# Hybrid attention and mLSTM block: who splits the attention's keys and queries into parts, and when they are stored

## The chip, the cores and the metric

One core of one Trainium2 chip runs the kernel. The time is the device time of one execution in microseconds; the median of several executions is compared.

## The reference

One layer on a sequence of 512 rows of width 1024. The input is normalised, multiplied by a wide matrix (1024 x 4616) and the product is split into nine groups of 512 columns (attention queries, keys, values and gate; mLSTM queries, keys, values, output gate and gate) and 8 gate columns. Cut to what matters:

```python
h = rms_norm(x, pre_norm_g[l])
proj = jnp.einsum('bsd,dc->bsc', h, w_in[l])
aq, ak, av, az, mq, mk, mv, mo, mz, mi, mf = split_columns(proj)
ya = moba_attention(partial_rope(att_heads(aq), pos), partial_rope(att_heads(ak), pos), att_heads(av))
ya = rms_norm(ya, attn_out_g[l]) * jax.nn.silu(az)
qk = jax.nn.silu(causal_depthwise_conv(jnp.concatenate([mq, mk], axis=-1), conv_w[l], conv_b[l]))
hm = mlstm_chunkwise(...)
ym = jax.nn.sigmoid(mo) * hm * jax.nn.silu(mz)
y = jnp.einsum('bsc,cd->bsd', jnp.concatenate([ya, ym], axis=-1), w_out[l])
x = x + rms_norm(y, post_norm_g[l])
```

Attention has 8 heads of 64; with this length every query sees all earlier rows. The mLSTM has 4 heads of 128.

## The kernel before

Every product is done in two parts of each operand: a high part, which is the number rounded to what TensorE reads, and a low part, which is the rest. A product is then three matmuls, high x high, high x low, low x high (`product`, L1497 to L1499, or in another order). For weights, ScalarE copies the raw tile into `w_hi` (`cut`, L817) and VectorE subtracts it from the raw tile to get `w_lo` (`cut`, L1068). GpSimd does this subtraction for the weight slots from 64 on (L662, L666).

The work is ordered by slots, written out by hand. A slot is one weight tile of 128 x 512: 88 in all. SyncE issues the load of slot n into one of 4 raw buffers once the low part of slot n-4 is done. ScalarE and VectorE run a loop over b and cut slot b+6 in step b. TensorE multiplies slot b in step b. So SyncE's slot n comes at about the time of VectorE's step n-10. Slots 0 to 7 are the mLSTM values. Then, for each head of the mLSTM, come four slots with its queries and keys (from 8, 20, 32 and 44) and eight slots of the attention: gate (12 to 19), keys (24 to 31), queries (36 to 43), values (48 to 55). `PARTS_AT` is (36, 48), the first slot behind the keys' and the queries' group and the next head's four. From slot 56 come the mLSTM gates, and with slot 62 the attention begins.

Around the change these things run in each head h of the mLSTM:

- VectorE: `conv_in` and `conv` (L1160, L1171, L1173 three times) for the head's queries (n = 2h) and keys (n = 2h+1), `qk_low(n)` (L1182) after ScalarE's silu (L884) and high copy (L888), `weighted(h, j)` (L1193), which reads the scores of tile j from PSUM and multiplies by the decay, `pm_low` (L1202), `head_sum` (L1210), `head_stats` (L1222 to L1234) and `head_norm` (L1240, L1242).
- TensorE: `head_scores(h, j)`, three matmuls after slots `ST_AT[h] + j` (40 to 43 for head 2, 52 to 55 for head 3), of 512, 384, 256 and 128 columns. It waits for `qk_low(2h+1)` and for `weighted` of the tile before. `head_values` in the four slots behind.
- GpSimd: `decay_rows(h)` (four DMAs, L641), `head_rsqrt(n)` (L624, the root for two tiles, for which `head_norm` waits), `decay_mask(h)` (four small additions, L648).

The attention's keys and queries: `kq_rows(w, m)` (w = 0 keys, 1 queries; m = 0 to 3 blocks of dimensions; L1253 to L1261) takes the projection out of PSUM, with the rotation for m = 0, into `by_dims`, which is the tile `stage`. ScalarE copies each to `by_dims_hi` (`kq_high`, L903), which is half of the tile `gy`. VectorE subtracts in place (`kq_low`, L1266). SyncE stores both parts to DRAM (`rows_out`, L528), and GpSimd's queue reads them back as `keys`, `queries` and `swapped` (L676, L685, L703, L706) in the arrangement that the attention needs. As queries use the same tiles as keys, `kq_rows(1, 0)` waits until all eight stores of the keys have landed (`kq_out[0]`).

Before, `PARTS_IN` says in which step the parts are taken, ScalarE one step ahead of VectorE, and SyncE stores them 11 slots behind:

```python
PARTS_IN = ({0: (0,), 2: (1,), 4: (2, 3)}, {4: (0, 1), 5: (2, 3)})
OUT_BEHIND = 11
```

ScalarE: m = 0 in step 35, 1 in 37, 2 and 3 in 39; queries 0 and 1 in 51, 2 and 3 in 52. VectorE: steps 36, 38, 40, 40 and 52, 52, 53, 53. SyncE: slots 47, 49, 51, 51 and 63, 63, 64, 64.

Of the kernel before, what the change touches and what calls it, by code (L numbers as in the profile page):

```python
# [18 lines left out]
F32 = mybir.dt.float32  # L19
F32R = mybir.dt.float32r  # L20
ALU = mybir.AluOpType
# [5 lines left out]
NT = SEQ // P  # L27
# [3 lines left out]
MH, MD = 4, 128  # L31
# [74 lines left out]
PE_ST = {ST_AT[h] + j: (h, j) for h in range(MH) for j in range(NT)}  # L106
PE_PV = {ST_AT[h] + NT + t: (h, t) for h in range(MH) for t in range(NT)}
PARTS_AT = (S_AQ, S_AV)
PARTS_IN = ({0: (0,), 2: (1,), 4: (2, 3)}, {4: (0, 1), 5: (2, 3)})
OUT_BEHIND = 11  # L110
FIRST_Q = 3
LAST_SLOT = S_MO - 2

# [109 lines left out]
def build(nc, x, pre_g, w_in, i_bias, f_bias, conv_w, conv_b, attn_g, mlstm_g, w_out, post_g, rope, out):  # L223
    with ExitStack() as ctx:
# [3 lines left out]
        def sem(name):  # L228
            return ctx.enter_context(nc.semaphore(name))
# [81 lines left out]
        by_dims, by_dims_hi = stage, gate.bitcast(F32R)  # L311
        by_dims_lo = stage[:].bitcast(F32R)
# [104 lines left out]
        conv_done = sem("conv_done")  # L417
# [33 lines left out]
        kq_hi = sem("kq_hi")  # L451
        kq_lo = sem("kq_lo")
# [42 lines left out]
        def low_done(eng, n):  # L495

            eng.wait_ge(w_lo_done[n % 2], n // 2 + 1)
# [4 lines left out]
        def turn_tile(n):  # L502

            _, kind, i = TURNS[n]
            return 0 if kind == "ym" else 4, NT - 1 - i
# [9 lines left out]
        @block.sync  # L515
        def _(sp):
            x2 = x.rearrange("b s d -> (b s) d")

            def load_x(c):
                k, n = X_CHUNKS[c]  # L520
                cols = slice(k * P, (k + n) * P)
                sp.dma_start(x_sb[:, :, cols], x2[:, cols].rearrange("(t p) d -> p t d", p=P)).then_inc(x_in[c], 16)

            def rows_out(w, m):

                for q, (done, src) in enumerate(((kq_hi, gate), (kq_lo, by_dims))):
                    sp.wait_ge(done, NT * w + m + 1)
                    sp.dma_start(kq_dram[w, :, q, ROT * m:ROT * m + ROT, :], src[:, m, :]).then_inc(kq_out[w], 16)  # L528

            for n, (mat, kind, k, c) in enumerate(SLOTS):  # L530
                if n in X_BEFORE:
                    load_x(X_BEFORE[n])
                if n >= RAW:
                    low_done(sp, n - RAW)
                w = w_in if mat == "in" else w_out
                if kind == "cols":
                    src = w[0, k * P:(k + 1) * P, c:c + AW]
                    dst = w_raw[:, n % RAW, :]
                else:
                    src = w[0, k * P:(k + 4) * P, c:c + MD].rearrange("(k p) c -> p k c", p=P)  # L540
                    dst = w_raw[:, n % RAW, :].rearrange("p (k c) -> p k c", k=4)
                sp.dma_start(dst, src).then_inc(raw_in[n % RAW], 16)
                if n == NK - 1:
                    sp.dma_start(wg_raw[:], w_in[0, :, MG:MG + 8].rearrange("(k p) c -> p k c", p=P)).then_inc(wg_in, 16)
                if n == S_QK + 6:
                    sp.wait_ge(ssx_done, NT)
                    sp.dma_start(gains[:], attn_g.to_broadcast([P, AW])).then_inc(gain_in, 16)
                for w in range(2):
                    for m in PARTS_IN[w].get(n - OUT_BEHIND - PARTS_AT[w], ()):
                        rows_out(w, m)  # L550
                if n == S_AQ + 4:
                    sp.wait_ge(az_gained, NT)
                    sp.dma_start(gains[:], mlstm_g.to_broadcast([P, AW])).then_inc(gain_in, 16)
            sp.wait_ge(kq_out[1], 32 * NT)
            sp.dma_start(post, post_g.to_broadcast([P, D])).then_inc(post_in, 16)

            def load_residual(i):
                t = NT - 1 - i
                sp.dma_start(xr[i], x2[t * P:(t + 1) * P, :]).then_inc(xr_in[i], 16)

            sp.wait_ge(ym_gated, NT)
            load_residual(0)
            load_residual(1)
            sp.wait_ge(turn_ps, TURN_OF["ym", NT - 1] + 1)
            load_residual(2)
            load_residual(3)
            store(sp, 0)
            store(sp, 1)
            store(sp, 2)
            sp.wait_ge(out_ready, 2 * NT - 1)  # L570
            sp.dma_start(out[0, 0:P, 0:AW], xr[NT - 1][:, 0:AW]).then_inc(out_done[NT - 1], 16)
            sp.wait_ge(out_ready, 2 * NT + 1)
            sp.dma_start(out[0, 0:P, quarter[1]], xr[NT - 1][:, quarter[1]]).then_inc(out_done[NT - 1], 16)
            for i in range(NT):
                sp.wait_ge(out_done[i], 32 + 16 * (i == NT - 1))
# [3 lines left out]
        def _(g):  # L579
# [43 lines left out]
            def rsqrt(dst, src):  # L623
                return g.tensor_tensor(dst, src, mhalf[:, 0:src.shape[1]], ALU.pow)  # L624
# [19 lines left out]
            def decay_mask(h):  # L644
                g.wait_ge(g_back, 16 * NT * (h + 1))
                for j in range(NT):
                    v = decay[j][:, 0:P]
                    g.tensor_tensor(v, v, causalT[:], ALU.add).then_inc(g_masked, 1)  # L648

            def head_rsqrt(n):  # L650
                g.wait_ge(var_done, n + 1)
                rsqrt(vr[:], vs2[:]).then_inc(vr_done, 1)

            def cut(n):
# [9 lines left out]
                else:  # L664
                    hi, lo = out_home(n - S_OUT)
                    g.tensor_tensor(lo, blocks(w_raw[:, n % RAW, :]), hi.bitcast(F32),  # L666
                                    ALU.subtract).then_inc(w_lo_done[n % 2], 1)

            def head_rows(w, h):

                return kq_dram[w, h].rearrange("q d s -> (q d) s")
# [47 lines left out]
            for h in range(1, MH):  # L719
                decay_rows(h)  # L720
                head_rsqrt(2 * h - 2)
                if h == MH - 1:
                    for n in range(AH):
                        keys_back(n)
                decay_mask(h)
                head_rsqrt(2 * h - 1)
            swapped_back(3)
            for h in range(FIRST_Q):
                queries_back(h)
# [76 lines left out]
        def _(a):  # L806
# [110 lines left out]
            for b in range(S_QK, LAST_SLOT + 1):  # L917
                if b == S_QK:
                    cut(b + AHEAD - 2)
                    cut(b + AHEAD - 1)  # L920
                if b == S_MZ + 1:
                    for t in range(NT):
                        v_high(t)
                cut(b + AHEAD)
                if b == S_QK:
                    a.wait_ge(onep_done, 1)
                    a.activation(rows[0], rows[2], ACT.Ln).then_inc(ln_done, 1)
                if b == S_QK + 1:
                    rope_scale()
                if b == S_QK + 5:  # L930
                    rope_evac()
                if b == S_QK + 3:
                    a.wait_ge(gmax_done, 1)
                    a.activation(gate_rows[32:48, :], rows[2], ACT.Copy, scale=-1.0).then_inc(gneg_done, 1)
                if b == ST_AT[0]:
                    a.wait_ge(aT_done, 1)
                    a.activation(emt[:], bank[7][:].rearrange("p (t c) -> p t c", t=NT)[:, :, 32:32 + MH],
                                 ACT.Exp).then_inc(emt_done, 1)
                for h in range(MH):
                    if b - 2 in PE_ST and PE_ST[b - 2][0] == h:  # L940
                        pm_high(*PE_ST[b - 2])
                    for c in range(2):
                        if b == S_Q[h] + 2 * c + 5:
                            conv_silu(2 * h + c)
                        if b == ST_AT[h] + c:
                            decays(h, 2 * c)
                            decays(h, 2 * c + 1)
                for c in range(2):
                    for t in (2 * c, 2 * c + 1):
                        if b == S_AK - 3 + c:  # L950
                            az_evac(a, t)
                for w in range(2):
                    for m in PARTS_IN[w].get(b + 1 - PARTS_AT[w], ()):
                        kq_high(w, m)

            def out_cut(n):
# [38 lines left out]
            for s in range(STEPS):  # L995
# [20 lines left out]
                for kind, what in events:  # L1016
# [7 lines left out]
                    elif kind == "y_sq":  # L1024
                        i, c = what
                        n = OUT_OF[i, c]
# [21 lines left out]
        def _(v):  # L1048
# [8 lines left out]
            def f32(ap):  # L1057
                return ap.bitcast(F32)
# [202 lines left out]
                v.tensor_tensor(by_dims[:, 0, :], by_dims[:, 0, :], turned, ALU.add).then_inc(kq_ready, 1)  # L1261
                v.wait_ge(kq_ready, NT * w + 1)

            def kq_low(w, m):
                v.wait_ge(kq_hi, NT * w + m + 1)
                v.tensor_tensor(by_dims_lo[:, m, :], by_dims[:, m, :], f32(by_dims_hi[:, m, :]),  # L1266
                                ALU.subtract).then_inc(kq_lo, 1)

            def v_low(t):
                part = v_hl[:, t * AH:(t + 1) * AH]  # L1270
                v.wait_ge(v_hi_done, t + 1)
# [4 lines left out]
            for b in range(S_QK, LAST_SLOT + 1):  # L1276
# [29 lines left out]
                for c in range(2):  # L1306
                    for m in (2 * c, 2 * c + 1):
                        if b == S_AQ - 3 + (m > 0):
                            kq_rows(0, m)
                        if b == S_AV - 3 + (m > 0):  # L1310
                            kq_rows(1, m)
                for w in range(2):
                    for m in PARTS_IN[w].get(b - PARTS_AT[w], ()):
                        kq_low(w, m)
                if b - 2 in PE_PV and PE_PV[b - 2][1] % 2 == 1:
                    head_stats(2 * PE_PV[b - 2][0] + PE_PV[b - 2][1] // 2)
                for h in range(MH):
# [562 lines left out]
```

## Time and profile before

| what | us |
|---|---|
| median of 3 runs | 322.23 (321.74 to 324.36) |
| the profiled execution, its own time | 323.46 |
| its span, first to last instruction | 321.5 |
| TensorE busy | 311.0 |
| VectorE busy | 224.6 |
| ScalarE busy | 163.0 |
| GpSimd busy | 109.2 |

The engines are PE (TensorE), DVE (VectorE), ACT (ScalarE), POOL (GpSimd) and SP (SyncE, which only issues DMAs). Times in the profile are microseconds from the start of the span. A busy engine is not always a bound one; the records of matmuls overlap, so the pace is read from their starts. The granted clock is 1.00 at TensorE's full speed and 0.50 at half of it.

### The profile page before, as it was taken

Reading aid. Unit: us, or ns where it says so; the run is one execution under the profiler, and the core shown is the slowest. Engines: PE = TensorE matmul, PEld = TensorE weight load, DVE = VectorE, ACT = ScalarE, POOL = GpSimd, SP = SyncE. Lnnn points to the kernel's source line nnn. Section 1 sums busy time; section 2 is a strip of 40 time slices with the busy share of each in tenths; the row PEclk is TensorE's granted clock in tenths of the full one; section 3 lists DMA queues with packets and bytes.
Section 4 is the critical chain, followed back from the end, with each engine's and each line's share of the span. In section 5 each row is a group of like instructions: output and inputs, shape, how many; then the busy total and the mean of one; then the engine's idle time right before and its main releaser. Section 6 shows DMA issues by size and latency. Waiting matters only on the chain.

```text
span 321.5 us, 4954 instructions
## 1 busy us (share of the span) xinstructions
PE 311.0 (97%) x1567; PEld 260.6 (81%) x1567; DVE 224.6 (70%) x508; ACT 163.0 (51%) x332; POOL 109.2 (34%) x144
## 2 busy tenths in 40 slices
PE   8999999999999999999998799999999999999992
PEld 4888888888888888888886688888888898888892
DVE  3544999658997799966997576654677586966534
ACT  4358947486373326742329261274566976452301
POOL 8201006228240231002550008796443888000000
PEclk9999999999999999999999599999999999999997
DMA  7931544863835563479583569591018376310111
GB/s 240 298 100 33 164 135 113 199 176 97 134 83 158 135 113 95 117 224 232 138 260 98 172 236 246 147 214 66 34 35 130 109 257 162 131 67 0 65 67 65
DMA packets 35576, 44.58 MB, mean 139 GB/s; under 512 B 3976, under 2 KB 19632, under 8 KB 35552
## 3 DMA queue, kind: packets, MB, share of 16 engines
q1 hardware_dynamic: 27360, 34.51, 35.2%
q0 software_dynamic: 8032, 9.63, 17.6%
q8 instruction: 13, 0.21, 0.3%
q10 hardware_dynamic: 160, 0.14, 0.1%
q14 instruction: 11, 0.09, 0.1%
HBM read 37.88 MB, written 6.39 MB: 138 GB/s over the span
## 4 chain that ended last, share of the span: by engine, by line
PE 71%; DVE 14%; issue 6%; DMA 4%; ACT 3%; SPq 1%; DVEq 0%; POOLq 0%; POOL 0%; ACTq 0%
PE bank L1497 18%; PE bank L1499 17%; PE bank L1498 17%; PE bank L1545 4%; DVE farena L1173 3%; PE bank L1830 3%; PE bank L1798 3%; DMA kq_rows<-stage 2%; DVE w_lo L1068 2%; PE bank L1779 2%; PE bank L1780 2%; DMA w_raw<-in_w_in 1%; PE bank L1729 1%; DVE stage L1253 1%; PE bank L1526 1%
## 5 line engine op out<-in xcount | busy, mean ns | idle before, releaser
L817 ACT ACTIVATE w_hi<-w_raw 128x512 fp32r<-128x512 f32 x71 | 43.7, 626 | 65.9 <-PE bank L1499 56.1
L1497 PE MATMUL bank<-w_hi,xT_hi 128*128 128x512 f32 (+1 forms) x180 | 73.3, 407 | 0.0
L1499 PE MATMUL bank<-w_hi,xT_lo 128*128 128x512 f32 (+1 forms) x180 | 70.7, 393 | 0.0
L1498 PE MATMUL bank<-w_lo,xT_hi 128*128 128x512 f32 (+1 forms) x180 | 70.3, 391 | 0.0
L1068 DVE TENSOR_TENSOR w_lo<-w_raw,w_hi 128x512 fp32r<-128x512 f32 x64 | 46.0, 729 | 8.7 <-ACT w_hi L817 8.6
L1497 PE MATMUL bank<-xT_hi,w_hi 128*128 128x512 f32 x128 | 50.8, 397 | 0.0
L1499 PE MATMUL bank<-xT_hi,w_lo 128*128 128x512 f32 x128 | 50.1, 392 | 0.0
L1498 PE MATMUL bank<-xT_lo,w_hi 128*128 128x512 f32 x128 | 50.0, 390 | 0.0
L1499 PEld LDWEIGHTS bank<-w_hi,xT_lo 128*128 128x128 f32 x180 | 34.4, 191 | 7.4
L1498 PEld LDWEIGHTS bank<-w_lo,xT_hi 128*128 128x128 f32 x180 | 34.6, 192 | 5.8
L1497 PEld LDWEIGHTS bank<-w_hi,xT_hi 128*128 128x128 f32 x180 | 34.5, 192 | 5.6
L1372 DVE CUSTOM_DVE_ANT_0 farena<-bank,causal 128x512 f32<-128x512 f32 (+3 forms) x32 | 15.7, 489 | 19.6 <-PE bank L1780 19.5
L1499 PEld LDWEIGHTS bank<-xT_hi,w_lo 128*128 128x128 f32 x128 | 24.0, 188 | 5.3
L1497 PEld LDWEIGHTS bank<-xT_hi,w_hi 128*128 128x128 f32 x128 | 24.1, 188 | 4.4
L1498 PEld LDWEIGHTS bank<-xT_lo,w_hi 128*128 128x128 f32 x128 | 24.1, 188 | 4.4
L993 ACT ACTIVATE rarena<-bank 128x512 fp32r<-128x512 f32 (+3 forms) x32 | 13.9, 434 | 20.1 <-PE bank L1830 20.0
L1378 DVE TENSOR_TENSOR rarena<-bank,rarena 128x512 fp32r<-128x512 f32 (+3 forms) x32 | 15.6, 487 | 6.3 <-ACT rarena L993 5.6
L641 POOL DMA_DIRECT2D farena<-g_rows x16 | 9.0, 568 | 31.3 <-DVE farena L1193 29.6
L1173 DVE SCALAR_TENSOR_TENSOR farena<-farena,pcol 128x512 f32<-128x512 f32 x24 | 18.4, 769 | 0.8
L985 ACT ACTIVATE farena<-farena,mx 128x512 f32<-128x512 f32 (+3 forms) x32 | 17.9, 560 | 1.1 <-DVE mx L1372 1.0
L1193 DVE SCALAR_TENSOR_TENSOR farena<-bank,farena 128x512 f32<-128x512 f32 (+3 forms) x16 | 7.8, 488 | 14.9 <-PE bank L1499 14.9
L624 POOL TENSOR_TENSOR vr<-vs,mhalf 128x2 f32<-128x2 f32 x8 | 5.7, 712 | 34.7 <-DVE vs L1232 34.7
(217 smaller groups left out, 613.4 us busy)
## 6 DMA issues: line engine op xcount, KB each, us to landing
w_raw<-in_w_in SPq DMA_DIRECT2D x72, 256.0 KB, 3.3
rarena<-kq_rows POOLq DMA_DIRECT2D x20, 256.0 KB, 4.5
w_raw<-in_w_out SPq DMA_DIRECT2D x16, 256.0 KB, 2.8
kq_rows<-gy SPq DMA_DIRECT2D x8, 256.0 KB
kq_rows<-stage SPq DMA_DIRECT2D x8, 256.0 KB
gy<-in_x SPq DMA_DIRECT2D x4, 512.0 KB, 3.9
out_y<-gy SPq DMA_DIRECT2D x7, 256.0 KB, 2.0
farena<-in_x SPq DMA_DIRECT2D x4, 256.0 KB, 4.2
```

What stands on the lines that cost most here:

```text
L817: a.activation(hi, raw, ACT.Copy).then_inc(w_hi_done, 1)
L985: a.activation(prob[:, s % 2, 0:n], sm[:, s % 2, 0:n], ACT.Exp, scale=-1.0, bias=mx[:, s:s + 1], accum_out=rsum[:, s:s + 1]).then_inc(prob ...
L993: a.activation(pT[:, 2 * (u % 2), 0:n], bank[4 + u % 2][:, 0:n], ACT.Copy).then_inc(pt_hi, 1)
L1068: v.tensor_tensor(lo, raw, hi, ALU.subtract).then_inc(w_lo_done[n % 2], 1)
L1173: ins = v.scalar_tensor_tensor(out=acc, in0=u[:, j:j + SEQ], scalar=tap[j], in1=acc, op0=ALU.mult, op1=ALU.add)
L1372: v.tensor_tensor_reduce(sm[:, s % 2, 0:n], bank[6 + s % 2][:, 0:n], causal[:, SEQ - n:], -Q_SCALE, BIG, ALU.add, ALU.min, mx[:, s:s + 1]) ...
L1378: v.tensor_tensor(pT[:, 2 * (u % 2) + 1, 0:n], bank[4 + u % 2][:, 0:n], f32(pT[:, 2 * (u % 2), 0:n]), ALU.subtract).then_inc(pt_lo, 1)
L1497: pe.matmul(o, hi, m_hi, start=start, stop=False)
L1498: pe.matmul(o, hi, m_lo, start=False, stop=False)
L1499: return pe.matmul(o, lo, m_hi, start=False, stop=stop)
L1545: mm = pe.matmul(bank[t][:], xs[:, k, t * P:(t + 1) * P], ws, start=k + term == 0, stop=False)
L1798: mm = pe.matmul(bank[2][:, 2 * P * (u % 2):2 * P * (u % 2 + 1)], v_hl[:, j * AH + h, :], pT[:, 2 * (u % 2):2 * (u % 2) + 2, j * P:(j + 1) ...
```

## The change

The high parts are taken by ScalarE in steps given by `HIGH_IN`: keys in 34 (m = 0) and 35 (1, 2, 3), queries in 47 (0, 1) and 48 (2, 3). The low parts are taken by GpSimd: for keys, m = 0 to 2 behind the mask of head 2 and m = 3 behind the root that follows; for queries all four, once the last convolution is done. The stores go out at SyncE's slots in `OUT_IN`: keys 46, 47, 47, 48, queries 61, 61, 62, 62.

```diff
-PARTS_IN = ({0: (0,), 2: (1,), 4: (2, 3)}, {4: (0, 1), 5: (2, 3)})
-OUT_BEHIND = 11
+HIGH_IN = ({-2: (0,), -1: (1, 2, 3)}, {-1: (0, 1), 0: (2, 3)})
+OUT_IN = ({10: (0,), 11: (1, 2), 12: (3,)}, {13: (0, 1), 14: (2, 3)})
@@ sync
-                    for m in PARTS_IN[w].get(n - OUT_BEHIND - PARTS_AT[w], ()):
+                    for m in OUT_IN[w].get(n - PARTS_AT[w], ()):
                         rows_out(w, m)
@@ gpsimd
+            def kq_low(w, m):
+                g.wait_ge(kq_hi, NT * w + m + 1)
+                g.tensor_tensor(by_dims_lo[:, m, :], by_dims[:, m, :], by_dims_hi[:, m, :].bitcast(F32),
+                                ALU.subtract).then_inc(kq_lo, 1)
...
                 decay_mask(h)
+                if h == MH - 2:
+                    for m in range(NT - 1):
+                        kq_low(0, m)
                 head_rsqrt(2 * h - 1)
+                if h == MH - 2:
+                    kq_low(0, NT - 1)
+            g.wait_ge(conv_done, 2 * MH)
+            for m in range(NT):
+                kq_low(1, m)
             swapped_back(3)
@@ scalar
-                    for m in PARTS_IN[w].get(b + 1 - PARTS_AT[w], ()):
+                    for m in HIGH_IN[w].get(b - PARTS_AT[w], ()):
                         kq_high(w, m)
@@ vector
-            def kq_low(w, m):
-                v.wait_ge(kq_hi, NT * w + m + 1)
-                v.tensor_tensor(by_dims_lo[:, m, :], by_dims[:, m, :], f32(by_dims_hi[:, m, :]),
-                                ALU.subtract).then_inc(kq_lo, 1)
...
-                for w in range(2):
-                    for m in PARTS_IN[w].get(b - PARTS_AT[w], ()):
-                        kq_low(w, m)
```

## Rows read from the trace of the kernel before

**Rows 1.** The page: busy time of the engines, and the chain that ended last.

```profile
PE 311.0 (97%) x1567; PEld 260.6 (81%) x1567; DVE 224.6 (70%) x508; ACT 163.0 (51%) x332; POOL 109.2 (34%) x144
...
PE 71%; DVE 14%; issue 6%; DMA 4%; ACT 3%; SPq 1%; DVEq 0%; POOLq 0%; POOL 0%; ACTq 0%
```

**Rows 2.** Stages: length, busy PE, PEld, DVE, ACT, POOL, granted clock, DMA share, GB/s.

```profile
176.00:178.00 2.00, 0.16 (x1) 0.00 (x0) 1.69 (x3) 1.49 (x4) 0.00 (x0) 1.00 0.01 2
178.00:179.00 1.00, 0.05 (x1) 0.08 (x1) 1.00 (x3) 0.16 (x1) 0.00 (x0) 0.60 0.92 229
179.00:184.00 5.00, 5.00 (x13) 4.13 (x14) 2.16 (x4) 1.51 (x3) 0.00 (x0) 0.50 0.63 200
```

**Rows 3.** Timeline of PE: start, duration; in brackets idle time before, and its releaser.

```profile
134.93 0.39 PE L1497 MATMUL bank<-rarena 128*128 128x512 f32 x1
...
138.36 0.34 PE L1497 MATMUL bank<-rarena 128*128 128x384 f32 x1
...
141.62 0.28 PE L1497 MATMUL bank<-rarena 128*128 128x256 f32 x1
...
172.44 0.50 PE L1497 MATMUL bank<-rarena 128*128 128x512 f32 x1 [0.19 <-DVE rarena L1182]
...
178.95 0.66 PE L1497 MATMUL bank<-rarena 128*128 128x384 f32 x1 [2.78 <-DVE farena L1193]
...
185.11 0.28 PE L1497 MATMUL bank<-rarena 128*128 128x256 f32 x1
```

**Rows 4.** The chain that ended last, in order of time: start, length, what.

```profile
140.05 8.00 DMA kq_rows<-stage
...
174.71 1.04 ACT gy L903 x2
```

**Rows 5.** Timeline of DVE from 145 to 179.

```profile
145.77 0.68 DVE L1068 TENSOR_TENSOR w_lo<-w_raw,w_hi 128x512 fp32r<-128x512 f32 x1
148.24 0.69 DVE L1258 TENSOR_TENSOR stage<-bank,farena 128x512 f32<-128x512 f32 x1 [1.79 <-DMA kq_rows<-stage]
...
166.95 2.33 DVE L1173 SCALAR_TENSOR_TENSOR farena<-farena,pcol 128x512 f32<-128x512 f32 x3
...
171.71 0.68 DVE L1182 TENSOR_TENSOR rarena<-farena,rarena 128x512 fp32r<-128x512 f32 x1
...
176.31 0.69 DVE L1068 TENSOR_TENSOR w_lo<-w_raw,w_hi 128x512 fp32r<-128x512 f32 x1 [2.11 <-ACT w_hi L817]
176.91 1.29 DVE L1266 TENSOR_TENSOR stage<-stage,gy 128x512 fp32r<-128x512 f32 x2
```

**Rows 6.** Groups by line and shape: count, busy us, mean ns, idle before.

```profile
L1266 DVE TENSOR_TENSOR stage<-stage,gy 128x512 fp32r<-128x512 f32 x8 | 5.2, 684 | 0.0
...
L662 POOL TENSOR_TENSOR w_lo<-w_raw,w_hi 128x512 fp32r<-128x512 f32 x8 | 10.4, 1327 | 0.4 <-ACT w_hi L817 0.4
```

**Rows 7.** Timelines of POOL and DVE where both work in SBUF.

```profile
73.46 6.00 POOL L718 TENSOR_TENSOR silu_az<-silu_az,gains 128x512 f32<-128x512 f32 x4 [4.67 <-ACT silu_az L786]
...
75.09 1.78 DVE L1068 TENSOR_TENSOR w_lo<-w_raw,w_hi 128x512 fp32r<-128x512 f32 x1
...
78.23 1.77 DVE L1068 TENSOR_TENSOR w_lo<-w_raw,w_hi 128x512 fp32r<-128x512 f32 x1
...
195.80 2.62 DVE L1224 SCALAR_TENSOR_TENSOR den<-num,emt 128x2 f32<-128x2 f32 x1
...
195.81 2.58 POOL L662 TENSOR_TENSOR w_lo<-w_raw,w_hi 128x512 fp32r<-128x512 f32 x2
```

**Rows 8.** Timelines of POOL and DVE around both parts.

```profile
118.34 2.78 POOL L648 TENSOR_TENSOR farena<-farena,causalT 128x128 f32<-128x128 f32 x4
...
133.40 0.68 DVE L1182 TENSOR_TENSOR rarena<-farena,rarena 128x512 fp32r<-128x512 f32 x1
...
192.76 1.44 POOL L703 DMA_DIRECT2D wg<-kq_rows  x2 [26.43 <-DMA kq_rows<-stage]
```

**Rows 9.** Timeline of SP: the first store of the queries' parts.

```profile
177.40 0.59 SPq L528 DMA_DIRECT2D kq_rows<-gy  x1
```

## The prediction, with its working

> **What bounds the kernel now.** I read the page's busy shares and its chain first, then the stages by window, then the timelines of the four engines around the one place where TensorE stands still. TensorE is busy for 97% of the span and is 71% of the chain that ended last [rows 1]. Its products leave it at an even pace from the first weights to the last, so only two things can shorten the run: fewer products (the change removes none), or fewer waits and slow-clock stretches of TensorE. The stages show one such place [rows 2]: from 176 to 178 TensorE is busy for 0.16 of 2 us, in 178 to 179 the granted clock goes from 1.00 to 0.60, and from 179 to 184 it is 0.50, the lower of its two levels (1.2 instead of 2.4 GHz).
>
> The timeline of TensorE gives the prices [rows 3]. It waits 0.19 us before the scores of head 3, tile 0 (at 172.44, for VectorE's `qk_low`), and 2.78 us before the scores of tile 1 (at 178.95, for VectorE's `weighted`). The stretch from there to the scores of tile 2 took 185.11 - 178.95 = 6.16 us at the lower clock; the same products for head 2, at the higher one, took 141.62 - 138.36 = 3.26 us. So the clock cost 2.90 us, and the place as a whole 0.19 + 2.78 + 2.90 = 5.87 us. That is what can be had.
>
> Why is VectorE late there? The chain of waits [rows 4] goes back through ScalarE's weight copy and, in front of it, its last two `kq_high` copies (174.71), and further back through VectorE without a gap to 148.24, where VectorE had waited 1.79 us for the last store of the keys to land [rows 4, 5] (issued by SyncE, 8.00 us until it landed). `kq_rows(1, 0)` can't overwrite the shared tile before that. Close to the stall VectorE idled 2.11 us at 176.31 for ScalarE's weight copy and then did two `kq_low` ahead of `weighted` [rows 5].
>
> **The change, part by part.** Times are those of the profiled execution: span 321.5, its own time 323.46, so 1.96 lie around the span. The median of the runs shown is 322.23, 1.23 less; I put the differences on that median.
>
> ScalarE's eight `kq_high` are issued sooner: the first part in schedule slots 34 and 35 instead of 35, 37 and 39, the second in 47 and 48 instead of 51 and 52. None is added. At the new places ScalarE mostly waits for TensorE to free a weight buffer, so they cost nothing there; if that cover were gone they would cost 0.6 us each. The last two stood in the chain in front of the weight copy for 1.04 us [rows 4], and two more stood before the same head's silu table and decays; that goes. With the DMA wait gone as well, I expect the copy that VectorE waited for some 3 us sooner (2 x 1.04 and part of the 1.79), so the wait of 2.11 us goes whole.
>
> VectorE's eight `kq_low` go: 0.68 us each as a record, 0.6 by start to start [rows 5, 6]. Two stood between the keys' rows and `qk_low` of head 2's keys, so 1.2 us come off that path. Four (the second part) stood between `qk_low(7)` and `weighted(3, 0)`: 2.4 us.
>
> SyncE's stores: by slot number they are only 1 to 3 slots sooner for the first part (46, 47, 48 for 47, 49, 51) and 2 sooner for the second (61, 62 for 63, 64); the same sixteen DMAs. The first part's last store was issued at 140.05 [rows 4]. Slot 48 comes when VectorE has cut slot 44's weights, which stands two operations ahead of `qk_low(5)` at 133.40 [rows 8]: 132 plus whatever VectorE is late, say 134; GpSimd must have cut block 3 as well, about 130. So the last store is issued at about 136 and lands, with the same 8.00 us, at 144, before 146.4, when VectorE is through the cut at 145.77 [rows 5]. The 1.8 us wait goes. What is late next is nothing: VectorE is busy without a gap until 169.28, so the end of the last convolution moves from there (166.95 + 2.33) to 167.5 [rows 5]. The weight loads of SyncE behind the stores move by the width of four issues (0.6 us each), in front of ScalarE's copies that are six slots ahead: nothing. The second part's stores went out from 177.4 on [rows 9]; now from about 173. GpSimd's reloads of queries follow sooner, and TensorE didn't wait for them before, so that is worth nothing either.
>
> GpSimd's eight `kq_low`. A subtraction of that size takes it 1.33 us [rows 6], so 4 x 1.3 = 5.2 us for each part. GpSimd has the time: it idles for 26.43 us up to 192.76 [rows 8]. Behind them in its queue stand the root for head 1 (between the third and the fourth) and, for the second part, only reloads that wait for these very parts. The cost is elsewhere. While GpSimd multiplied four tiles at 73.46, VectorE's subtractions took 1.78 and 1.77 us instead of 0.69 [rows 7]: 1.1 us lost for each GpSimd operation that meets a VectorE operation with two inputs in SBUF. At 195.80 a VectorE operation on two columns took 2.62 us, the whole of two GpSimd subtractions (2.58) [rows 7]. So a moved part costs VectorE between 0 (when VectorE is idle or reads one input) and 1.3 us, against 0.6 saved. I take 1.1, since these are the same operations on the same sizes.
>
> The Trainium skill has this as a rule, and it speaks against the change (SBUF, State Buffer, section "Who interferes with whom"): the second port pair of VectorE is GpSimd's, it is an exclusive lock, and a VectorE instruction with two SBUF inputs and a GpSimd instruction that reads SBUF block each other, whichever comes second for the whole length of the first. The trace agrees in kind; by the rule's whole length the price would be 1.3 us per operation, 5.2 us per part instead of 4.4.
>
> Second part, where it decides. `kq_low(1, .)` waits for the last convolution, 167.5, and so starts in the very moment when VectorE has `qk_low(6)`, a normalisation, two weight cuts and `qk_low(7)` to do: 3.1 us from 169.28 to 172.39 before [rows 5]. Now 167.5 + 3.1 = 170.6 without contention. TensorE wants `qk_low(7)` at 172.44 - 0.19 = 172.25 [rows 3], so there are 1.65 us of slack. Four operations at 1.1 are 4.4; about 0.75 of that lies beside the normalisation, which reads one tile. 170.6 + 3.65 = 174.25: TensorE waits 2.0 us before the scores of tile 0. (Bounds: 0, if GpSimd loses each race, and 170.6 + 5.2 - 172.25 = 3.5.) The next wait, for `weighted`, goes: TensorE came to it 178.95 - 2.78 - 172.44 = 3.73 us after the start of the first scores [rows 3], so now at 178.0, and VectorE, with two cuts at 0.6 in front, is there at 175.5.
>
> First part: GpSimd is free when the masks of head 2 are done (118.34 + 2.78 = 121.1), three subtractions follow, the fourth after the root at about 129 [rows 8]. VectorE there has convolutions (two SBUF inputs) but also reductions from PSUM and statistics; laying the two timelines side by side I get 2.4 us of the 4.4. Less the 1.2 saved, `qk_low(5)` ends 1.2 later than its 134.08 (133.40 + 0.68) [rows 8]; TensorE asks at 134.93 [rows 3]. So a new wait of 0.35 us (bounds 0 and 5.2 - 1.2 - 0.85 = 3.2).
>
> Sum: waits 0.35 + 2.0 = 2.35 instead of 2.97. And the clock? It fell when TensorE had stood for about 2.2 us (last product done at about 176.2, fall in the slice 178 to 179) [rows 2, 3], and it did not fall after 0.19. A wait of 2.0 is shorter than what had passed when it fell, so I take it that the clock stays, by a narrow margin. Then 5.87 - 2.35 = 3.5 us are gained: 318.7 (own time of a profiled execution about 320).
>
> **The rivals.**
> A, the wait is only moved and the clock falls again: 0.35 + 2.0 + 2.9 = 5.25 against 5.87, so -0.6: 321.6. For it: the margin of the clock is 0.2 us. Against: the shorter wait.
> B, contention is small because GpSimd's reads fall into VectorE's gaps and one-input operations: no wait, no slow clock, -5.9: 316.4. For it: 1.65 us of slack and the 2.11 us of idle VectorE; against: the dense stretch after the convolution.
> C, the port decides the other way, in the first part: if VectorE loses more than 2.05 us (1.2 saved + 0.85 slack) between 121 and 134, TensorE waits there; at the whole 4.4 that is 2.35 us, with the clock falling 2.9 more, and the second part, with nothing beside the normalisation, at 170.6 + 4.4 - 172.25 = 2.8, and again 2.9. 10.95 against 5.87: +5.1, 327.3, slower. For it: the one operation that was held up by two. Against: the reductions and statistics between.
> D, the change doesn't do what it says: the keys' last store still lands too late, since by slots it is only three sooner and behind GpSimd's root. Then the 1.8 us stay and all of the second part is later by it: 0.35 + 3.8 + 2.9 = 7.05, +1.2: 323.4. Against: some 2 us of margin.
>
> **How the numbers follow.** Forecast 0.36, A 0.24, B 0.24, C 0.10, D 0.06. A measurement of this kernel tells about 1%, 3.2 us, from no change. Faster by more than that (below 319.0): all of B and three quarters of the forecast, 0.51. Slower (above 325.5): most of C and a little of D, 0.10. Within: 0.39. The range 316.0 to 323.0 holds the forecast, A and B with a little on both sides, and leaves out C and half of D.
>
> **What would show it.** Right: the wait for the DMA at `kq_rows(1, 0)` is gone; GpSimd's eight subtractions have 1.3 to 1.8 us each; VectorE's `w_lo` cuts beside them have 1.1 us more than 0.69; TensorE waits some 2 us for `qk_low(7)` (line of head scores) and no longer for `weighted`; the granted clock stays 1.00 there. Wrong: VectorE's records around 168 to 174 no longer than before (then B); a TensorE wait near 135, or the clock at 0.50 there (C); VectorE still waiting for a DMA near 147 (D). A wait of TensorE after 200 that isn't there now would upset all of it.

## The result, and the profile after

The changed kernel takes 325.54 us (median of 13 executions, 324.36 to 328.18), the kernel before 322.21 beside it (13 executions). The ratio is 1.0109, with an interval of 1.0081 to 1.0136: slower by 1.1%. The forecast was 318.7, faster. Ratios here and below leave out executions more than 1.5% above the fastest of their kernel, among them one of e10 that took 796.13 us, 2.5 times as long as its others, for a reason that no run shows.

In the profiled executions the span went from 321.5 to 323.6 us, and the own time from 323.46 to 325.68. TensorE's timeline after the change answers to [rows 3]. The columns are start and duration, and in brackets the idle time before and who ended it.

```profile
136.85 0.50 PE L1502 MATMUL bank<-rarena 128*128 128x512 f32 x1 [1.83 <-DVE rarena L1195]
...
141.98 0.34 PE L1502 MATMUL bank<-rarena 128*128 128x384 f32 x1
...
178.57 0.58 PE L1502 MATMUL bank<-rarena 128*128 128x512 f32 x1 [2.69 <-DVE rarena L1195]
...
183.70 0.34 PE L1502 MATMUL bank<-rarena 128*128 128x384 f32 x1
```

There are now two places instead of one. Both are the first scores of a head (2 and 3), and both wait for `qk_low` (L1195, was L1182). The wait of 2.78 us for `weighted` is gone. The granted clock fell in both places, as its rows by stage show (columns as in [rows 2]):

```profile
137.00:138.00 1.00, 1.00 (x5) 0.83 (x6) 0.40 (x1) 1.00 (x3) 0.00 (x0) 0.94 0.81 307
138.00:141.00 3.00, 3.00 (x9) 2.32 (x8) 1.29 (x2) 1.65 (x5) 0.00 (x0) 0.50 0.68 223
141.00:143.00 2.00, 2.00 (x11) 1.69 (x10) 0.98 (x2) 0.79 (x2) 0.00 (x0) 0.92 0.89 257
176.00:178.00 2.00, 0.00 (x0) 0.00 (x0) 2.00 (x3) 0.89 (x3) 0.76 (x1) 1.00 0.00 0
178.00:179.00 1.00, 0.43 (x2) 0.35 (x3) 1.00 (x2) 0.00 (x0) 0.00 (x0) 0.93 0.57 117
179.00:181.00 2.00, 2.00 (x6) 1.59 (x5) 1.68 (x4) 0.87 (x2) 0.00 (x0) 0.50 0.83 260
```

Each place takes 5.13 us from its first scores to the scores of the next tile (141.98 - 136.85 and 183.70 - 178.57). The same work at full clock took 138.36 - 134.93 = 3.43 us for head 2 [rows 3], and for head 3 as much in e9 below (172.71 to 176.14). So each clock fall cost 1.70 us, and the two places together cost 1.83 + 1.70 + 2.69 + 1.70 = 7.92 us. The one place before cost 5.87. The difference, 2.05, is the whole of what the span grew by (2.1). The medians differ by 3.3. The profiled execution of before lay 1.25 above its median, that of after 0.14 above, and the remaining 1.2 us are in executions of which there is no trace. The likely reason is the clock. The profiled execution of before had a mean granted clock of 0.984, lower than any of the 52 executions of that kernel that were run beside the experiments (0.988 to 0.996), while that of after, 0.987, lies among its own kernel's (0.984 to 0.993). So an ordinary execution of before probably lost less than the 5.87 us of this trace. That is argued from the means, which also hold the last few us of each span, at 0.50, and is not shown by a trace.

Why is `qk_low` late? VectorE's timeline up to it, in both places:

```profile
121.53 1.25 DVE L1253 TENSOR_TENSOR hsc<-vr,iden 128x2 f32<-128x2 f32 x1
122.82 2.53 DVE L1255 TENSOR_SCALAR gy<-num,mva,hsc 128x128 f32<-128x128 f32 x2
...
129.82 1.50 DVE L1184 TENSOR_SCALAR farena<-farena,pcol 128x512 f32<-128x512 f32 x1
...
168.96 2.33 DVE L1186 SCALAR_TENSOR_TENSOR farena<-farena,pcol 128x512 f32<-128x512 f32 x3
171.20 0.69 DVE L1195 TENSOR_TENSOR rarena<-farena,rarena 128x512 fp32r<-128x512 f32 x1
171.81 1.25 DVE L1253 TENSOR_TENSOR hsc<-vr,iden 128x2 f32<-128x2 f32 x1
173.10 2.52 DVE L1255 TENSOR_SCALAR gy<-num,mva,hsc 128x128 f32<-128x128 f32 x2
175.54 2.37 DVE L1081 TENSOR_TENSOR w_lo<-w_raw,w_hi 128x512 fp32r<-128x512 f32 x2
177.84 0.68 DVE L1195 TENSOR_TENSOR rarena<-farena,rarena 128x512 fp32r<-128x512 f32 x1
```

And GpSimd's at the same times:

```profile
121.03 4.24 POOL L671 TENSOR_TENSOR stage<-stage,gy 128x512 fp32r<-128x512 f32 x3
...
129.74 1.30 POOL L671 TENSOR_TENSOR stage<-stage,gy 128x512 fp32r<-128x512 f32 x1
...
171.37 5.40 POOL L671 TENSOR_TENSOR stage<-stage,gy 128x512 fp32r<-128x512 f32 x4 [3.03 <-DVE farena L1186]
```

A multiplication of two columns (L1253) takes 1.25 us instead of 0.15. The two normalisations behind it (L1255) take 2.53 and 2.52 as a pair instead of 0.60. Two weight cuts take 2.37 instead of 1.29, one step of the convolution (L1184) 1.50 instead of 0.55. The sum of the excess is 1.10 + 1.93 + 0.95 = 3.98 us for the keys' four subtractions and 1.10 + 1.92 + 1.08 = 4.10 us for the queries' four: 1.0 us each. Beside it VectorE saved 0.6 us each, but only two of the eight had stood ahead of `qk_low(5)`, and none ahead of `qk_low(7)`: 1.2 us saved against 3.98 in the first place, nothing against 4.10 in the second.

What the change was meant to undo did go. No row is left in which VectorE waits for the keys' store [rows 5]: after the change `kq_rows(1, 0)` starts at 150.00, straight behind the weight cut. The end of head 3's last convolution is at 171.29, where it was at 169.28, with TensorE 3.5 us later by then: 1.5 us sooner against TensorE.

### The profile page after: what moved, and what is told of

Its sections match the earlier page's. It is cut to its first block, busy times and chain, and to the rows that moved or that the text cites. A ratio compares the mean times of both kernels' runs of the same rounds, so it can differ in the third digit from the quotient of the medians.

```text
span 323.6 us, 4955 instructions
## 1 busy us (share of the span) xinstructions
PE 311.9 (96%) x1567; PEld 260.9 (81%) x1567; DVE 227.9 (70%) x500; ACT 163.0 (50%) x332; POOL 120.9 (37%) x152
## 4 chain that ended last, share of the span: by engine, by line
PE 76%; DVE 17%; issue 5%; DVEq 0%; ACT 0%; POOLq 0%; POOL 0%; ACTq 0%
PE bank L1502 19%; PE bank L1504 19%; PE bank L1503 19%; PE bank L1550 4%; DVE farena L1186 3%; PE bank L1835 3%; DVE w_lo L1081 3%; PE bank L1803 3%; DVE gy L1255 2%; PE bank L1784 2%; PE bank L1785 2%; PE bank L1531 1%; PE bank L1734 1%; DVE farena L1184 1%; PE bank L1517 1%
## 5 line engine op out<-in xcount | busy, mean ns | idle before, releaser
L1081 DVE TENSOR_TENSOR w_lo<-w_raw,w_hi 128x512 fp32r<-128x512 f32 x64 | 47.0, 747 | 13.4 <-ACT w_hi L830 13.3
L1504 PE MATMUL bank<-xT_hi,w_lo 128*128 128x512 f32 x128 | 50.8, 397 | 0.0
L1503 PE MATMUL bank<-xT_lo,w_hi 128*128 128x512 f32 x128 | 50.7, 396 | 0.0
```

The lines of the kernel that those rows point to most:

```text
L1081: v.tensor_tensor(lo, raw, hi, ALU.subtract).then_inc(w_lo_done[n % 2], 1)
L1503: pe.matmul(o, hi, m_lo, start=False, stop=False)
L1504: return pe.matmul(o, lo, m_hi, start=False, stop=stop)
```

## The experiments

Theory 1 says that VectorE is held up by GpSimd's subtractions, at the two points where TensorE waits for `qk_low`. Theory 2 says that the earlier stores and copies cost the time: SyncE or ScalarE is held up, and the weights come late. The kernel before stood at 322.77 beside e1 to e4, at 322.86 beside e5 to e8, and at 322.33 beside e9 and e10 (medians).

**e1: all low parts back on VectorE; early high parts and early stores kept.**

```diff
+LOW_IN = ({0: (0,), 1: (1, 2), 2: (3,)}, {3: (0, 1), 4: (2, 3)})
@@ vector
+                for w in range(2):
+                    for m in LOW_IN[w].get(b - PARTS_AT[w], ()):
+                        kq_low(w, m)
@@ gpsimd: the calls of kq_low taken out
```

> The changed kernel with its early high parts and early stores kept, and all eight low parts back on VectorE (keys in steps 36, 37, 37, 38, queries in 51, 51, 52, 52). Theory 1 (the loss is VectorE held up by GpSimd's subtractions, just before qk_low of heads 2 and 3): TensorE's two waits of 1.83 and 2.69 us and both clock falls go; two more low parts than before stand ahead of qk_low(5), 1.2 us against 0.85 us of slack, so a wait of about 0.35 us there: 322.2 - 5.87 + 0.35 = 316.7. Theory 2 (the loss comes from the earlier stores and copies: SyncE or ScalarE is held up and the weights come late): the time stays near 325.5 and VectorE's records have no excess.

319.58 us, ratio 0.9892 (0.9831 to 0.9953). So the change without its move to GpSimd is faster than before by 1.1%, and that same move makes it slower than before. Theory 2 falls as an account of the loss. The forecast was 3 us too low, and TensorE's timeline shows one part of that, a wait I had not seen:

```profile
135.65 0.50 PE L1503 MATMUL bank<-rarena 128*128 128x512 f32 x1 [0.26 <-DVE rarena L1188]
...
184.75 0.47 PE L1503 MATMUL bank<-w_hi,xT_hi 128*128 128x512 f32 x1 [1.24 <-DVE rarena L1278]
```

The 0.26 us were expected (0.35). The 1.24 us are TensorE waiting for the low parts of the attention's values (L1278), and ScalarE's timeline has what is in front of them (the first row is the weight copy of slot 62, the second the values' copies):

```profile
182.31 0.63 ACT L823 ACTIVATE w_hi<-w_raw 128x512 fp32r<-128x512 f32 x1 [3.79 <-DMA w_raw<-in_w_in]
...
183.15 2.41 ACT L913 ACTIVATE rarena<-bank,rx 128x512 fp32r<-128x512 f32 x4
```

ScalarE waits 3.79 us for the weights of slot 62, whose load was issued behind the queries' stores, and the values' copies (L913) stand behind that. Theory 2 has this much in it: the earlier queries' stores do cost something. These two waits are 1.5 of the 2.9 us. The rest is about what the base was off: the forecast took 5.87 us, from an execution 1.25 us above its median, off a median.

**e2: only the keys' low parts back on VectorE; e3: only the queries'.**

```diff
+LOW_IN = ({0: (0,), 1: (1, 2), 2: (3,)}, {})          # e2
+LOW_IN = ({}, {3: (0, 1), 4: (2, 3)})                 # e3
```

> As e1, but only the keys' low parts on VectorE; the queries' on GpSimd as in the change. Theory 1: only the wait before the scores of head 3 is left, 2.7 us, with a clock loss of 1.7 to 2.9 us: 316.7 + 4.4 to 5.6 = 321.1 to 322.3. Theory 2: near 325.5, as nothing is changed in stores and copies.

> As e1, but only the queries' low parts on VectorE; the keys' on GpSimd as in the change. Theory 1: only the wait before the scores of head 2 is left, 1.8 us, with a clock loss of 1.7 to 2.9 us: 322.2 - 5.87 + 3.5 to 4.7 = 319.8 to 321.0. Theory 2: near 325.5.

e2: 323.82 us, ratio 1.0020 (0.9984 to 1.0057). e3: 322.86, ratio 0.9988 (0.9949 to 1.0026). They lie 1.5 and 1.9 us above the upper end of what theory 1 expected, and both between the change and e1: each part is enough to lose what the rest gains. The traces have the waits where they should be. For e2 (first fence) head 3's scores wait for `qk_low`, and head 2's for only 0.25 us, as in e1. For e3 (second) only head 2's wait. The second wait in each is the one for the values' low parts. It explains a part of why both are above what I expected:

```profile
175.64 0.50 PE L1506 MATMUL bank<-rarena 128*128 128x512 f32 x1 [2.45 <-DVE rarena L1191]
189.34 0.77 PE L1506 MATMUL bank<-w_hi,xT_hi 128*128 128x512 f32 x1 [3.32 <-DVE rarena L1281]
```

```profile
137.31 0.50 PE L1508 MATMUL bank<-rarena 128*128 128x512 f32 x1 [1.84 <-DVE rarena L1193]
187.67 0.47 PE L1508 MATMUL bank<-w_hi,xT_hi 128*128 128x512 f32 x1 [1.16 <-DVE rarena L1283]
```

In e3 the clock fell at the first of its waits (0.50 from 139 to 141). In e2 it did not fall at the wait of 2.45 us, but at that of 3.32. This trace of e2 is of an execution of 327.17 us, 3.35 above the median, so the size of its second wait is not taken as usual.

**e4: no subtraction at all.**

```diff
-                g.tensor_tensor(by_dims_lo[:, m, :], by_dims[:, m, :], by_dims_hi[:, m, :].bitcast(F32),
-                                ALU.subtract).then_inc(kq_lo, 1)
+                g.memset(by_dims_lo[:, m, 0:1].bitcast(F32), 0.0).then_inc(kq_lo, 1)
```

> As the change, but GpSimd writes one column in place of each low part (the low parts of keys and queries are left out of the computation), so neither VectorE nor GpSimd subtracts. Theory 1: all waits of TensorE and both clock falls go, 322.2 - 5.87 = 316.3, and that is the most that moving these parts can bring. Theory 2: near 325.5.

318.62 us, ratio 0.9858 (0.9795 to 0.9922). This is as far as moving these eight subtractions can go with the stores of the change, and it is 2.3 us above what I expected. e1, which does all eight on VectorE, is only 1.0 us above it. So on VectorE they cost next to nothing once they don't stand in front of `qk_low` in a bad moment; on GpSimd they cost 7.5 us: the change is 3.33 us above the kernel before that ran beside it, e4 is 4.15 below its own. (The 1.0 us between e1 and e4 is within the spread of their four executions each.) e4 still has waits of 0.45 us for the values' low parts and 0.9 in the attention, and its miss, like that of e1, is mostly the base.

**e5: GpSimd writes for about as long as it did, but reads nothing.** Each subtraction (1.3 us) becomes two writes of zeros (0.53 us each).

```diff
-                g.tensor_tensor(by_dims_lo[:, m, :], by_dims[:, m, :], ..., ALU.subtract).then_inc(kq_lo, 1)
+                g.memset(by_dims_lo[:, m, :].bitcast(F32), 0.0).then_inc(kq_wr, 1)
+                g.wait_ge(kq_wr, NT * w + m + 1)
+                g.memset(by_dims_lo[:, m, :].bitcast(F32), 0.0).then_inc(kq_lo, 1)
```

> As the change, but each subtraction of GpSimd is replaced by two writes of zeros over the same low part, about 0.5 us each (the low parts of keys and queries are left out of the computation): GpSimd writes SBUF for about 1 us per part and reads nothing. Theory 1a (VectorE's operations with two inputs lose against GpSimd's reads, its normalisations and tensor_scalar lose because they take both of the second ports, the writing one too): the weight cuts beside it keep 0.69 us, and the two normalisations stay longer than 0.60. Theory 1b (the normalisations lost against the reads as well): everything on VectorE is as long as without GpSimd, and the time is that of the kernel without low parts, about 319.

317.99 us (one execution), as if GpSimd did nothing. VectorE beside six of the writes (121.2 to 124.5) and beside eight (167.9 to 172.3):

```profile
121.74 0.15 DVE L1255 TENSOR_TENSOR hsc<-vr,iden 128x2 f32<-128x2 f32 x1
121.92 1.01 DVE L1257 TENSOR_SCALAR gy<-num,mva,hsc 128x128 f32<-128x128 f32 x2
...
123.38 0.68 DVE L1083 TENSOR_TENSOR w_lo<-w_raw,w_hi 128x512 fp32r<-128x512 f32 x1
...
168.51 0.61 DVE L1257 TENSOR_SCALAR gy<-num,mva,hsc 128x128 f32<-128x128 f32 x2
169.05 1.28 DVE L1083 TENSOR_TENSOR w_lo<-w_raw,w_hi 128x512 fp32r<-128x512 f32 x2
```

The operations with two inputs keep 0.15 and 0.68 us. The normalisations have 1.01 in one place and 0.61 in the other, so they meet GpSimd's writes at times, at 0.4 us for a pair. Theory 1a holds for its first half and only in part for the second. For operations with two inputs it is GpSimd's reading that costs. For the normalisations the runs leave open how much is due to the reading and how much to the length of one GpSimd instruction, 1.3 us against 0.53. The Trainium skill (SBUF, State Buffer, section "Who interferes with whom") names both kinds: an instruction with two SBUF inputs contends with a GpSimd instruction that reads SBUF and not with one that only writes it, and `tensor_scalar` can enter a mode with two ports, in which it contends with GpSimd, if its operands meet that mode's conditions. The rows of the change and of e5 agree with the first, and in kind with the second; that the mode was on here, no row says. It is what I passed over when I counted the normalisation as free.

**e6: the queries' subtractions on GpSimd, but later.** As e2, with another wait and the stores behind it.

```diff
-            g.wait_ge(conv_done, 2 * MH)
+            g.wait_ge(pm_done, NT * (MH - 1) + 1)
-OUT_IN = (..., {13: (0, 1), 14: (2, 3)})
+OUT_IN = (..., {17: (0, 1), 18: (2, 3)})
```

> As e2 (keys' low parts on VectorE, queries' on GpSimd), but GpSimd waits until the first weighted scores of head 3 are there, instead of the end of the last convolution, and the queries' stores go out at SyncE's slots 65 and 66. Theory 1 (the moment decides, not the engine): the same four subtractions meet a VectorE that idles in part, TensorE no longer waits for qk_low(7), and the time is about 4 us below e2's 323.8, that is 319 to 320. Rival: GpSimd's subtractions hold up weighted and pm_low of the next tiles instead, and the time stays at 322 or more.

325.68 us, ratio 1.0100 (1.0074 to 1.0127): some 6 us above what I expected. The trace says that the first half of the theory held and that the stores' delay undid it. VectorE lost here too (its cut took 1.78 us, the first row), but TensorE did not wait for it. Apart from 0.3 us before head 2's scores, TensorE waits only at its first attention scores:

```profile
179.61 1.78 DVE L1077 TENSOR_TENSOR w_lo<-w_raw,w_hi 128x512 fp32r<-128x512 f32 x1
...
203.71 1.22 DVE L1249 TENSOR_TENSOR hsc<-vr,iden 128x2 f32<-128x2 f32 x1 [11.42 <-POOL vr L625]
```

```profile
197.31 1.45 POOL L709 DMA_DIRECT2D wg<-kq_rows  x2 [16.46 <-DMA kq_rows<-stage]
...
202.88 0.73 POOL L625 TENSOR_TENSOR vr<-vs,mhalf 128x2 f32<-128x2 f32 x1
```

```profile
207.32 0.79 PE L1788 MATMUL bank<-rarena 128*128 128x512 f32 x1 [4.58 <-DVE num L1219]
```

GpSimd waits until 197.31 for the queries' stores to land, since its queue has the reload there; behind the reload stands the root of head 3, at 202.88. VectorE waits 11.42 us for that root, and TensorE 4.58 for VectorE. The clock fell there too, before TensorE began again, and rose only at about 212, which comes on top of the wait:

```profile
206.00:211.00 5.00, 3.68 (x9) 2.91 (x10) 3.83 (x19) 0.44 (x1) 2.00 (x5) 0.50 0.35 103
```

So the queries' stores have a due time after all: not that of the scores, but that of what GpSimd has queued behind the reload.

**e7 and e8: everything on VectorE, the queries behind head 3's first weighted scores.**

```diff
+OUT_IN = ({11: (0,), 13: (1,), 14: (2, 3)}, {16: (0, 1), 17: (2, 3)})                    # e7
+OUT_IN = ({11: (0,), 13: (1,), 14: (2, 3)}, {16: (0,), 17: (1,), 18: (2,), 19: (3,)})    # e8
+LOW_IN = ({0: (0,), 2: (1,), 4: (2, 3)}, {6: (0, 1), 7: (2, 3)})
```

> No low parts on GpSimd. High parts early as in the change. Keys: low parts on VectorE in the steps of before (36, 38, 40, 40), the last stores one slot sooner than before (50). Queries: low parts on VectorE in steps 54 and 55, behind the first weighted scores of head 3, stores at slots 64 and 65. Expected if e1's remaining waits are what I read (0.26 us for qk_low(5) from two more low parts ahead of it; 1.24 us for the values' low parts, because the weights of slot 62 came 3.8 us late behind the queries' stores): both go, 319.6 - 1.5 = 318.1. If the values' wait is not due to the stores: 319.3.

> As e7, but the queries' stores are spread, one block per slot at 64, 65, 66 and 67, so that fewer stores stand ahead of each weight load. If the loads behind the stores matter in e7, 0.5 to 1 us less than e7; if not, the same.

321.73 us (ratio 0.9964, 0.9936 to 0.9992) and 323.89 (1.0050, 1.0020 to 1.0080). Both miss: e7 was expected at 318.1, and e8 at 0.5 to 1 us less than e7, where it is 2.2 more. The wait for the values is gone from both, as expected, but waits at the first attention scores take its place, as in e6 with its late reload, and they are longer with the spread. e8 also waits 1.73 us, at 220.97, for weights that GpSimd cuts (0.28 in e7). e7 is the first fence, e8 the second:

```profile
202.94 0.50 PE L1785 MATMUL bank<-rarena 128*128 128x512 f32 x1 [0.94 <-DVE num L1216]
213.93 0.48 PE L1785 MATMUL bank<-rarena 128*128 128x512 f32 x1 [1.19 <-DMA rarena<-kq_rows]
```

```profile
204.40 0.50 PE L1785 MATMUL bank<-rarena 128*128 128x512 f32 x1 [2.45 <-DVE num L1216]
```

**e9: the queries' stores between the two bounds.** As e1, with the queries' parts one step and their stores one slot later.

```diff
-OUT_IN = (..., {13: (0, 1), 14: (2, 3)})
-LOW_IN = (..., {3: (0, 1), 4: (2, 3)})
+OUT_IN = (..., {14: (0, 1), 15: (2, 3)})
+LOW_IN = (..., {4: (0, 1), 5: (2, 3)})
```

> As e1 (no low parts on GpSimd, keys as in e1), but the queries' low parts on VectorE in steps 52 and 53 as before the change, and their stores at SyncE's slots 62 and 63: behind the load of slot 62, which came 3.8 us late in e1 and held up the values' high parts, and soon enough for the reload not to hold up GpSimd's root, as it did in e7. Expected: e1's wait of 1.24 us for the values goes, nothing new comes: 319.6 - 1.2 = 318.4. If the values' wait has another cause, 319.6; if the reload is late already, 320 or more with a wait at the first attention scores.

318.79 us (317.60 to 319.46, 6 executions), ratio 0.9896 (0.9863 to 0.9929). The profiled execution is the fastest of them, with a span of 315.8. Stores at slots 62 and 63 are late enough for the weights of slot 62 (ScalarE's wait of 3.79 us for them is gone) and early enough for the reload. The low parts moved by one step as well, so what each of the two shifts did is not told apart. After the first 6 us, TensorE has one wait of 0.27 us left, and its stages at the old place are full, at full clock:

```profile
170.00:180.00 10.00, 10.00 (x48) 8.38 (x47) 7.98 (x15) 6.40 (x12) 0.00 (x0) 1.00 0.63 191
180.00:190.00 10.00, 10.00 (x50) 8.35 (x49) 6.71 (x15) 5.39 (x10) 2.14 (x4) 1.00 0.71 239
```

**e10 and e11: the kernel before, with ScalarE's early steps alone.**

```diff
+HIGH_IN = ({-2: (0,), -1: (1, 2, 3)}, {-1: (0, 1), 0: (2, 3)})
@@ scalar
-                    for m in PARTS_IN[w].get(b + 1 - PARTS_AT[w], ()):
+                    for m in HIGH_IN[w].get(b - PARTS_AT[w], ()):
```

> The kernel before with one edit: ScalarE takes the high parts in the early steps of the change; low parts (VectorE) and stores exactly where they were. It tells what the early high parts alone are worth. The keys' last store is as late as before, so VectorE's wait for it stays (1.8 us), but ScalarE's weight copy near the end is no longer behind four high copies: VectorE's idle 2.1 us at the weight cut goes, weighted(3, 0) comes about 2 us sooner, and TensorE's wait of 2.78 us shrinks below 1 us, and the clock stays: 322.2 - 2 - 2.9 = 317 to 318. If the early highs are worth nothing without the stores: 322.

> The same kernel as e10, for its trace, since e10's one profiled execution ran at a quarter of TensorE's pace throughout (796 us). By e10's time, 320.0, about 1 us more than expected at most: I expect one wait of TensorE left of 1 to 1.5 us, before the scores of head 3 or for the values' low parts, no clock fall in the middle, and VectorE's wait for the keys' store still there.

319.94 us (seven executions), ratio 0.9926 (0.9898 to 0.9954); e11, the same kernel for its trace, took 319.38 (one execution). So 2.4 of the 3.5 us that e9 gains, two thirds, come from this one edit. The trace shows both waits where they were expected: TensorE's before the scores of tile 1 is down from 2.78 us to 0.74 with the clock staying up, less than the 1 to 1.5 us expected, and VectorE's for the keys' store is still there, the second row:

```profile
176.78 0.41 PE L1503 MATMUL bank<-rarena 128*128 128x384 f32 x1 [0.74 <-DVE farena L1199]
```

```profile
148.16 0.69 DVE L1264 TENSOR_TENSOR stage<-bank,farena 128x512 f32<-128x512 f32 x1 [1.35 <-DMA kq_rows<-stage]
```

## Why the prediction was wrong

What held: that one place holds the time that can be had (e9, which has none of its waits left, is 5.7 us shorter in the profiled executions, though only 3.5 in the medians); that the wait for the keys' store goes; that ScalarE's early copies shorten the path and cost nothing that shows (e10, e11); that the wait for `weighted` goes; that GpSimd's eight subtractions take 1.3 to 1.4 us each; that each takes about 1.1 us from VectorE where it meets it (1.0 measured).

What failed are three steps of the sum, all in the same direction. Together they are 5.6 of the 6.8 us by which the forecast was off.

1. "Laying the two timelines side by side I get 2.4 us of the 4.4", in the first part. VectorE lost 3.98 us. I took the normalisations and the convolution's `tensor_scalar` as operations with one input that GpSimd does not meet. Both met it (1.93 and 0.95 us). So `qk_low(5)` ended 2.7 us later than before instead of 1.2, and TensorE waited 1.83 us instead of 0.35: 1.5 us. That is the point of rival C (more than 2.05 us lost).
2. "About 0.75 of that lies beside the normalisation, which reads one tile", in the second part. That 0.75 was taken as free, and the normalisation alone lost 1.92: 4.10 us lost in all instead of 3.65, and a wait of 2.69 instead of 2.0, 0.7 us more.
3. "A wait of 2.0 is shorter than what had passed when it fell, so I take it that the clock stays." It fell after both, though one of them was only 1.83 us. In the row for 137 to 138 the clock is still 0.94 on average, so it fell at about 137.9, one us after TensorE had begun again. The two falls cost 3.40 us where the sum had nothing. The margin was misread as well: a mean of 0.60 in the slice 178 to 179 [rows 2] puts the fall at 178.2, which is 2.0 us after 176.17, where TensorE's wait began, and not 2.2. A wait forecast at 2.0 had no margin. And an idle time that has passed in one trace is no bound for the next.

The remaining 1.2 us are the base: the 5.87 us were read in an execution 1.25 us above its median and taken off the median.

The mechanism that decided is rival C's, which the prediction gave 0.10. Its price was too high: 10.95 us against the 7.92 measured, since I took the waits as 2.35 and 2.8 (1.83 and 2.69) and each fall as 2.90 (1.70). The step under it is one that I worked out and then set aside. Rival C had 4.4 us of loss per part, and the trace had no `tensor_scalar` beside GpSimd's 128x512 subtractions that would have priced it, so it should have been taken at its upper bound in the dense stretches, not at zero. The trace was not silent either. Six of the convolution's eight `tensor_scalar` steps before took 0.55 us; the two that took longer lie beside GpSimd's gate rows (48.16 to 50.42) and mask additions (118.34 to 121.1):

```profile
49.91 0.81 DVE L1171 TENSOR_SCALAR farena<-farena,pcol 128x512 f32<-128x512 f32 x1
...
118.38 0.69 DVE L1171 TENSOR_SCALAR farena<-farena,pcol 128x512 f32<-128x512 f32 x1
```

A term I had at "nothing" was not zero either: the weight loads behind the earlier stores. In e1 and e3 TensorE waits 1.2 us for the values' low parts, in e4 and e5 0.5. In the changed kernel ScalarE waits 2.66 us for a weight load ahead of the values' copies, but TensorE, late itself, does not wait for them.

## What to carry to other kernels

An engine that idles is no free place for work if its instructions hold up those of the busy one: here eight subtractions moved from VectorE to GpSimd freed 0.6 us each and cost 1.0 us each, and on the paths that TensorE waited for they freed 1.2 us in all and cost 8.1. Price such a move by the other engine's operations in exactly that stretch, small ones too, and count what TensorE's clock costs when the stretch is a path that it waits for. A large share of the gain was to be had by issuing the copies of a third engine earlier. And a store has a due time set by whatever is queued behind its reload, not only by the one who reads the data.

## What the runs showed that I had not expected

- Operations of VectorE that read a single tile were held up beside GpSimd's subtractions as long as those with two inputs: two normalisations of 128 columns took 2.53 us as a pair instead of 0.60. With GpSimd only writing, the pair took 1.01 or 0.61.
- Whether the clock falls does not go by the length of the wait alone. It fell around waits of 1.83 us (the change), 1.84 (e3) and 2.78 (before), and stayed at 1.00 through one of 2.45 us in e2 and one of 2.45 us in e8. Their stages show it, e2 first:

```profile
174.00:180.00 6.00, 4.36 (x20) 3.70 (x21) 4.18 (x8) 1.71 (x3) 0.00 (x0) 1.00 0.53 149
...
200.00:206.00 6.00, 3.55 (x16) 2.64 (x15) 5.22 (x16) 1.26 (x2) 2.81 (x3) 1.00 0.67 201
```

- A fall can be dear or cheap: 2.90 us in the profiled execution of before, 1.70 in each of the two after.
